# One 512-column product for the high weight instead of two of 256 columns, in five projections of a two-block transformer kernel

## The reference, cut to what matters

```python
# block 1
h = rms_norm(x, attn_norm_w[l])
proj = h @ w_cat                    # 2048 x 6448: "input projection"
y = concat([rwkv7_mixer(...), gdn_mixer(...)])
x = x + y @ w_out[l]
h = rms_norm(x, ffn_norm_w[l])
x = x + (jax.nn.silu(h @ ffn_w_gate[l]) * (h @ ffn_w_up[l])) @ ffn_w_down[l]   # gate/up: 2048 x 5632 each
# block 2
q, k, v, f_logit = split(h @ fox_w_in)        # 2048 x 6160: "fox projection"
...
up = h @ w_up                                  # 2048 x 11264
y = conv_b + conv_w[0]*pad(up)[t] + conv_w[1]*pad(up)[t+1] + conv_w[2]*pad(up)[t+2]
gate, val = split(y); out = (silu(gate) * val) @ w_down
```

## Time and profile before

| what | value |
|---|---|
| two timed runs | 2782.08 and 2787.71 us, median 2784.89 |
| the profiled execution | 2763.92 us, its span in the trace 2762.2 us, mean granted TensorE clock 0.959 of full |
| TensorE matrix products busy | 2625.6 us, 95% of the span |
| VectorE, ScalarE busy | 1494.2 us (54%), 1109.7 us (40%) |
| DMA | 421.74 MB, 153 GB/s over the span |

### The profile page before, as it was taken

One profiled execution on the slowest core, in us unless ns is written; L12 is line 12 of the kernel. 1 busy time (PEld: TensorE's weight loads), 2 busy tenths in 40 slices (PEclk: granted clock), 3 DMA queues, 4 the chain that ended last, 5 costly groups with the idle time before them and its releaser, 6 DMA issues.

```text
span 2762.2 us, 57089 instructions
## 1 busy us (share of the span) xinstructions
PE 2625.6 (95%) x24185; PEld 2545.2 (92%) x24185; DVE 1494.2 (54%) x1679; ACT 1109.7 (40%) x1050; POOL 69.2 (3%) x69
## 2 busy tenths in 40 slices
PE   7999988889899999999999799998999999999999
PEld 6999878478889999999999799986989999999999
DVE  5457567374554454444444544546456676676444
ACT  3333413231335444444333433434345555454333
POOL 1000040000100000000010000000100000000000
PEclk8999989679999999999999899997999999999999
DMA  5555200000545565555555356530545555566664
GB/s 164 188 190 186 91 2 4 1 1 27 170 153 188 194 197 189 192 197 190 193 193 178 102 196 196 188 118 1 172 160 188 196 196 187 193 197 189 193 197 153
DMA packets 169214, 421.74 MB, mean 153 GB/s; under 512 B 17462, under 2 KB 22139, under 8 KB 168859
## 3 DMA queue, kind: packets, MB, share of 16 engines
q1 hardware_dynamic: 168699, 419.13, 46.7%
q10 hardware_dynamic: 416, 1.18, 0.1%
HBM read 418.16 MB, written 2.10 MB: 152 GB/s over the span
## 4 chain that ended last, share of the span: by engine, by line
PE 88%; DVE 8%; ACT 2%; issue 1%; SPq 0%; DMA 0%; DVEq 0%; POOL 0%; ACTq 0%; POOLq 0%
PE ps L1581 25%; PE ps L1582 25%; PE ps L1583 25%; DVE LOW L879 1%; PE ps L1621 1%; PE ps L2001 1%; DVE NSQ L913 1%; ACT HIW L508 1%; PE ps L1671 1%; PE ps L1678 1%; PE ps L1705 1%; PE ps L1715 1%; PE ps L1734 1%; PE ps L1712 1%; PE ps L1969 1%
## 5 line engine op out<-in xcount | busy, mean ns | idle before, releaser
L879 DVE TENSOR_TENSOR LOW<-RAW,HIW 128x2048 fp32r<-128x2048 f32 (+2 forms) x400 | 910.4, 2276 | 1020.7 <-ACT HIW L508 1020.7
L1581 PE MATMUL ps<-H,HIW 128*128 128x256 f32 x4928 | 1373.7, 279 | 43.0 <-DVE LOW L879 21.2
L1582 PE MATMUL ps<-H,HIW 128*128 128x256 f32 x4928 | 1371.3, 278 | 0.0
L1583 PE MATMUL ps<-H,LOW 128*128 128x256 f32 x4928 | 1371.2, 278 | 0.0
L508 ACT ACTIVATE HIW<-RAW 128x2048 fp32r<-128x2048 f32 (+2 forms) x400 | 760.8, 1903 | 1202.1 <-PE ps L1583 1202.1
L1581 PEld LDWEIGHTS ps<-H,HIW 128*128 128x128 f32 x4928 | 936.0, 190 | 47.1 <-issue 26.1
L1582 PEld LDWEIGHTS ps<-H,HIW 128*128 128x128 f32 x4928 | 932.7, 189 | 0.0
L1583 PEld LDWEIGHTS ps<-H,LOW 128*128 128x128 f32 x4928 | 932.2, 189 | 0.0
L1581 PE MATMUL ps<-HID,HIW 128*128 (+1 forms) x1408 | 388.7, 276 | 1.3 <-DVE LOW L879 1.3
L1582 PE MATMUL ps<-HID,HIW 128*128 (+1 forms) x1408 | 388.6, 276 | 0.0
L1583 PE MATMUL ps<-HID,LOW 128*128 (+1 forms) x1408 | 388.6, 276 | 0.0
(11 more groups left out here) (351 smaller groups left out, 1787.7 us busy)
## 6 DMA issues: line engine op xcount, KB each, us to landing
RAW<-in_ffn_w_up SPq DMA_DIRECT2D x264, 512.0 KB, 4.5
RAW<-in_ffn_w_down SPq DMA_DIRECT2D x176, 512.0 KB, 4.6
RAW<-in_w_in SPq DMA_DIRECT2D x96, 512.0 KB, 4.2
RAW<-in_fox_w_in SPq DMA_DIRECT2D x96, 512.0 KB, 4.3
RAW<-in_ffn_w_gate SPq DMA_DIRECT2D x88, 512.0 KB, 3.8
RAW<-in_w_out SPq DMA_DIRECT2D x32, 512.0 KB, 4.9
RAW<-in_fox_w_out SPq DMA_DIRECT2D x32, 512.0 KB, 4.9
RAW<-in_w_in SPq DMA_DIRECT2D x4, 576.0 KB, 4.9
```

Source lines behind the costliest of these rows:

```text
L879: V.tensor_tensor(LOW[:, u_const % 4, 0:n], RAW[:, u_const % 4, 0:n], HIW[:, u_const % 2, 0:n].bitcast(F32), ALU.subtract).then_inc(lo_mad ...
L1581: mm(o_, hi_w, h_hi, start=start, stop=False)
L1582: mm(o_, hi_w, h_lo, start=False, stop=False)
L1583: i = mm(o_, lo_w, h_hi, start=False, stop=stop)
```

## The change

In the phases whose `group_phase` has `both=True` (IN, FOX, FFN1, FFN2), the first two products of a triple become one: the high weight tile is loaded once and meets the high and the low half of the activation tile in one product of 512 columns over the whole bank. The low weight by the high activation goes into the second half of the bank. The output tile is then the sum of the bank's two halves. For this H and HID are laid out with the two halves of a k-tile side by side. OUT, OUT2, both down projections and the small units keep three products.

The evictions change with it: ScalarE copies the second half of each bank to SBUF (`small_half`), VectorE adds the first half to it (`add_half`) and frees the bank. FFN1's silu and product, which were part of the eviction, become whole-group instructions behind units 1 and 2 (silu on ScalarE, product on VectorE), HID's parts follow behind units 3 and 4. In FFN2 tap 0 moves from VectorE to ScalarE (behind unit 1, 8 instructions with a scale and a bias per partition), the 16 instructions of the other two taps are dealt 5, 6 and 5 to units 2, 3 and 4, the silu moves to unit 5, the product to 6 and both parts of HID to 7. Two scratch tiles (ROWS, RWK) move to another place in H's memory.

```diff
-        H = at("H", [P, 2, KT, T], h0, F32R); o += 32768
+        H = at("H", [P, KT, 2, T], h0, F32R); o += 32768
...
-        HID = at("HID", [P, 2, FT, T], r2, F32R)
+        HID = at("HID", [P, FT, 2, T], r2, F32R)
...
+            def small_half(dst, f, m0, u_end, z0, g):
+                if f < GROUP - 1:
+                    act.wait_ge(tile_summed, g * 7 + (m0 + f + 1))
+                else:
+                    act.wait_ge(unit_used, g * UG + (u_end + FREE_UNITS))
+                A(dst, ps[f][:, T:2 * T], ACT.Copy).then_inc(half_out, 1)
+
+            def evac_in(g):
+                for f in range(GROUP):
+                    small_half(PR[:, bass.ds(g * 8 + (3 + f), 1), PAD:TP], f, M_IN, U_IN + UG, Z_IN, g)
...
-            group_phase(U_IN, 3)
+            group_phase(U_IN, 3, evac_in)
...
             def evac_ffn1(g):
-                for i in range(4):
-                    act.wait_ge(tile_summed, g * 7 + (M_FFN1 + 2 * i + 1))
-                    A(SG[:, i, :], ps[2 * i][:, 0:T], ACT.Silu).then_inc(S("gate_act"), 1)
+                act.wait_ge(S("hid_made"), g + 1)
+                for f in range(GROUP):
+                    small_half((SG, HS)[f % 2][:, f // 2, :], f, M_FFN1, U_FFN1 + UG, Z_FFN1, g)
 
             def tail_ffn1(g, j):
                 if j == 1:
-
-                    act.wait_ge(bank_freed, g * 8 + (N_FFN1 + 8 + FREE_BANKS))
-                    A(HID[:, 0, bass.ds(g * 4, 4), :], HS[:], ACT.Copy).then_inc(S("hid_hi"), 1)
+                    act.wait_ge(bank_freed, g * 8 + (N_FFN1 + 7 + FREE_BANKS))
+                    A(SG[:], SG[:], ACT.Silu).then_inc(S("gate_act"), 1)
+                elif j == 3:
+                    act.wait_ge(S("hid_full"), g + 1)
+                    A(HID[:, bass.ds(g * 4, 4), 0, :], HS[:], ACT.Copy).then_inc(S("hid_hi"), 1)
...
             def tail_ffn2(g, j):
-                if j == 3:
+                if j == 1:
+                    act.wait_ge(bank_freed, g * 8 + (N_FFN2 + 8 + FREE_BANKS))
+                    cb = COL["ffn_conv_b_2"]
+                    for i in range(GROUP):
+                        row = (i % 2) * FT + i // 2
+                        ins = A((YG, YV)[i % 2][:, i // 2, :], UC[:, i, 0:T], ACT.Identity,
+                                scale=vec[:, bass.ds(g * 4 + (COL["conv0"] + row), 1)],
+                                bias=vec[:, bass.ds(g * 4 + (cb + row), 1)])
+                    ins.then_inc(S("conv_step"), 1)
+                elif j == 5:
                     act.wait_ge(S("conv_step"), g * 3 + 3)
                     A(YG[:], YG[:], ACT.Silu).then_inc(S("conv_gate"), 1)
...
+            def add_half(dst, f, z0, g):
+                dve.wait_ge(half_out, g * 8 + (z0 + f + 1))
+                V.tensor_tensor(dst, dst, ps[f][:, 0:T], ALU.add).then_inc(bank_freed, 1)
+
             def evac_in(g):
                 for f in range(GROUP):
-                    summed(2, f, U_IN + UG, g)
-                    V.tensor_copy(PR[:, bass.ds(g * 8 + (3 + f), 1), PAD:TP], ps[f][:, 0:T])\
-                        .then_inc(bank_freed, 1)
+                    add_half(PR[:, bass.ds(g * 8 + (3 + f), 1), PAD:TP], f, Z_IN, g)
...
             def tail_ffn2(g, j):
-                if j in (1, 2):
-                    dve.wait_ge(S("conv_step"), g * 3 + j)
-                    for i in range(GROUP):
-                        ins = V.scalar_tensor_tensor(y(i), UC[:, i, j:j + T], tap(g, j, i), y(i), ALU.mult, ALU.add)
-                    ins.then_inc(S("conv_step"), 1)
-                elif j == 4:
+                if j in (2, 3, 4):
+                    if j == 2:
+                        dve.wait_ge(S("conv_step"), g * 3 + 1)
+                    for n in range((0, 5, 11)[j - 2], (5, 11, 16)[j - 2]):
...
-                        h_hi, h_lo = hcol(0, k), hcol(1, k)
+                        h_both = hcol(k)
+                        h_hi, h_lo = h_both[:, 0, :], h_both[:, 1, :]
                         start, stop = first and kk == 0, last and kk == len(tiles) - 1
-                        o_ = ps[f][:, 0:T]
-                        mm(o_, hi_w, h_hi, start=start, stop=False)
-                        mm(o_, hi_w, h_lo, start=False, stop=False)
-                        i = mm(o_, lo_w, h_hi, start=False, stop=stop)
+                        if both:
+                            mm(ps[f][:, :].rearrange("p (a t) -> p a t", a=2), hi_w, h_both, start=start, stop=False)
+                            i = mm(ps[f][:, T:2 * T], lo_w, h_hi, start=False, stop=stop)
+                        else:
+                            o_ = ps[f][:, 0:T]
+                            mm(o_, hi_w, h_hi, start=start, stop=False)
+                            mm(o_, hi_w, h_lo, start=False, stop=False)
+                            i = mm(o_, lo_w, h_hi, start=False, stop=stop)
```

More of the change, by code:

```diff
@@ L693, in _ @@
             got("ya_full")
-            A(H[:, 0, 0:PAIRS, :], BH[:], ACT.Copy).then_inc(S("mix_hi"), 1)
+            A(H[:, 0:PAIRS, 0, :], BH[:], ACT.Copy).then_inc(S("mix_hi"), 1)
             got("cols_made")
@@ L735, in _ @@
             got("yb_full")
-            A(H[:, 0, PAIRS:KT, :], OG[:], ACT.Copy).then_inc(S("mix_hi"), 1)
+            A(H[:, PAIRS:KT, 0, :], OG[:], ACT.Copy).then_inc(S("mix_hi"), 1)
             def ffn_phase(u0, evac, tail):
@@ L1559, in _, with h_in, hid_in, unit @@
             mm = nc.tensor.matmul
-            def h_in(part, k):
-                return H[:, part, k, :]
-            def unit(u, tiles, nf, wcol, first=False, last=False, g=None, step=0, n0=None, hcol=h_in, h_wait=None):
+            def h_in(k):
+                return H[:, k, :, :]
+            def hid_in(k):
+                return HID[:, k, :, :]
+            def unit(u, tiles, nf, wcol, first=False, last=False, g=None, step=0, n0=None, hcol=h_in, h_wait=None, both=False):
                 v = u + 1
@@ L1593, in gate_up_col, with group_phase @@
                 return kk * 1024 + (i % 2) * 512 + (i // 2) * P
-            def group_phase(u0, n0, groups, wcol=plain, k_norm=None, h_wait={}):
+            def group_phase(u0, n0, groups, wcol=plain, k_norm=None, h_wait={}, both=True):
                 with pe.Fori(0, groups) as g:
@@ L1598, in group_phase @@
                         hw = h_wait.get(j) if k_norm is None else (S("h_made"), 8 * HN[k_norm] + j + 1)
-                        unit(u0 + j, [2 * j, 2 * j + 1], GROUP, wcol, j == 0, j == UG - 1, g, UG, n0, h_wait=hw)
+                        unit(u0 + j, [2 * j, 2 * j + 1], GROUP, wcol, j == 0, j == UG - 1, g, UG, n0, h_wait=hw, both=both)
             def down(u0, n0, made0):
@@ L1606, in down @@
                         unit(b + j, [2 * j, 2 * j + 1], GROUP, plain, j == 0, n0=n0 + 8 * half,
-                             hcol=lambda part, k: HID[:, part, k, :], h_wait=(S("hid_made"), made0 + 10))
+                             hcol=hid_in, h_wait=(S("hid_made"), made0 + 10))
                     with pe.Fori(0, 4) as i:
@@ L1610, in down @@
                             unit(b + 2 + j, [4 + 2 * j, 5 + 2 * j], GROUP, plain, g=i, step=4,
[L1611 removed]
+                                 hcol=lambda k: HID[:, bass.ds(i * 8 + k, 1), :, :].rearrange("p k a t -> p (k a) t"))
                     for j in range(18, 22):
                         unit(b + j, [2 * j, 2 * j + 1], GROUP, plain, last=j == 21,
[L1614 removed]
+                             hcol=hid_in, h_wait=(S("hid_made"), made0 + 11))
             def norm(k, presummed=True):
@@ L1951, in _ @@
             got("yb_full")
-            group_phase(U_OUT, N_OUT, 2, h_wait={0: (S("mix_made"), 1), 4: (S("mix_made"), 2)})
+            group_phase(U_OUT, N_OUT, 2, h_wait={0: (S("mix_made"), 1), 4: (S("mix_made"), 2)}, both=False)
             norm(1)
@@ L2042, in _ @@
             got("att_made", 2)
-            group_phase(U_OUT2, N_OUT2, 2)
+            group_phase(U_OUT2, N_OUT2, 2, both=False)
             norm(4)
```

88 lines of the change are left out of this document (46 added, 42 removed).

## The result

| | before | after |
|---|---|---|
| timed runs | 2782.08, 2787.71 us | 2826.32, 2827.93 us |
| median | 2784.89 us | 2827.12 us |
| profiled execution, its span | 2763.92, 2762.2 us | 2826.32, 2824.6 us |

The ratio after to before is 1.0152, 95% interval 1.0106 to 1.0197: slower by 1.5% where 1.6% faster was forecast. The second is the fairer one. Over the 70 single runs of the kernel before in this document its median is 2763.5 us, and only 15 of the 70 are as slow as the two timed runs of the table.

The account below looks back on a forecast made before the run. TensorE's stream of products was taken to bound the kernel. Cheaper triples save 45.3 us, phase ends cost 2; 43.3 us off the median 2784.89 gives 2741 us, 1.6% less, range 2716 to 2772.

Parts of the forecast that it names:

- What a triple costs after: TensorE in IN, FOX, FFN1, FFN2: 512-column product 216.3 ns plus 256-column product 113.3, together 329.6 instead of 340.
- The 6.6 ns beyond the columns: Time of a 256-column product in FFN1 above its 106.7 ns of columns, read as pacing by weight loads.
- The three float32 measurements: Plain float32 products of 512, 256 and 64 columns, starting 0.43 us, 215.6 ns and 111 ns apart.
- The 111 ns of 64-column products: Distance of plain float32 products with full weight tiles, taken as the pace that weight loading sets.
- the term: Saving on TensorE in the four both=True phases: 4352 triples x 10.4 ns = 45.3 us.
- The bounds: Limits for the new triple on TensorE: 323 ns (gain 17), 333.2 (gain 6.8), or 340 (no gain).
- (e): Rival: on TensorE a 512-column float32r product runs as two of 256 with two loads, 340 ns; 2787 us; 5%.
- (a): Rival: TensorE's weight loads were hidden already, so dropping one saves only 10 to 29 us; 2758 to 2777 us; 14%.
- (b): Rival: at 34 group ends the helpers cost up to 0.5 us each, 17 us; about 2758 us; 12%.
- (d): Rival: ScalarE's copies at group ends become the bottleneck, slower; at 0.65 us per copy about 2804 us; 5%.
- The count of triples: IN, FOX, FFN1 and FFN2: 34 groups of 8 units of 16 triples, 4352 triples.
- the point named as the test: FFN1's loop in the profile after: 512-column product followed after 216 ns, the 256-column one after 113.

Follow-up runs that it names:

- The second: The changed kernel, unchanged, measured again against the kernel before: 2823.34 us against 2760.05, ratio 1.0224.
- runs 3: Products alone, no kernel, in widths of 256 to 512 columns: 113.3 ns for 256, 233.2 for 512, triple 340.0, pair 353.3.
- run 4: Products alone, no kernel, activations moved by 0 to 512 bytes: pairs 346.6 to 353.5 ns, triples 353.3 to 360.0; also 16-column weight tiles and plain float32.
- run 8: Products alone, no kernel: bf16 215.8 and 109.2 ns, float32r with 16-column weight tiles 231.7 and 117.8; triples, low weights at 64 or 192, 340.0 in 47 of 48 starts.
- run 7: Products alone, no kernel, over 8 x 8 addresses of activations and low weights: mean 349.6 ns for pairs, 354.2 for triples, none under 340.0.
- 192: The kernel before with low weights 192 bytes past a multiple of 256 instead of 64, other tiles moved along; run twice, ratios 0.9962 and 0.9951.

## Why the prediction was wrong

**The failed step** is "What a triple costs after", from "I read them as paced by weight loads" to "takes 213.3 + 3 = 216.3 ns and hides the load of the low weight; the 256-column product behind it still takes 113.3". They took 235.0 and 118.3. The 6.6 ns beyond the columns are neither the weight load's nor the instruction's: they come with the columns of float32r (runs 3, 4, 8). The three float32 measurements were read correctly and run 4 repeats those of 512 and 256 columns; but plain float32 spends two clocks per column, and says nothing of a type that streams one column per clock. The 111 ns of 64-column products lay near 113.3 by accident, as far as the runs show: loads of half the duration made 256 columns no faster. Priced as measured, the term is 4352 x (340 - 353.3) = -57.9 us against the best pace, and -47.8 against the draw of the profiled run, in place of +45.3. The base of the sum was a draw as well: 2784.89 us was the median of two slow ones, 21 us above the kernel's usual 2763.5. Against that, the kernel after (2821.6 to 2827.9 us) is some 60 us slower. In the two profiled runs 47.8 us of it are the pairs and 17.5 us the untouched triples.

**The bounds were too narrow on one side.** The last of them, "no better than two, 340, no gain", excluded a loss without a row that did. The row existed: windows in IN at 117.2 ns would have shown that 340 was not the price of a triple but one of two, and would have set the lower end at 353, a loss.

**The rivals.** (e) had the sign of the wide product nearly right (no gain) but 340 for 353. (a) would have given 333 to 338 for the pair. The Trainium skill's rule (TensorE: Matmul & The Clock Gate, section Back-to-back issue gap: N/2.4 + 2.5 ns) would have given 325.0. By that rule bf16 products take 215.8 and 109.2, and run 8 measured exactly this; for float32r the runs have 226.7 to 235 and 113.3 to 118.3, and disagree. (b) and (d) didn't happen: no waits in the loops.

**What held.** The count of triples; that TensorE's stream sets the time; the evictions' distances within 0.1 us per instruction; nothing at the group ends in the loops (in FFN2 with the luck told above); and the point named as the test, the distance behind a 512-column product, which showed the error at a glance.

**What stays open.** Why float32r at one column per clock falls short by a sixteenth or more, and why by the address. Bf16 has half the bytes per column and float32 or the 1.2 GHz level half the columns per ns, and all three lose nothing that grows with the columns, which would suit a supply of 4-byte columns that can't quite keep up at 2.4 GHz; that is argued, not shown. Nor is it known what decides the draw after a pause, why 192 draws well in the kernel when it didn't differ from 64 in run 8, why triples at 0 and 64 took 340 in runs 3, 7 and 8 and 353.3 in run 4, and whether pairs would pay in a kernel at an address where triples don't reach 340.

## What to carry to other kernels

Before costing fewer, wider matrix products, measure the pair's distance at the kernel's own type and addresses: for float32r at 2.4 GHz, time goes by columns and addresses. Dropping instructions and weight loads bought nothing here against triples at their best address; against triples at most other addresses of run 7 it saved a few ns in 350. Read the distance between products in every phase of the trace, not in one; two paces in one trace mean that the price being improved on is a draw. When a kernel's runs spread by 1 to 2%, try its operands' offsets modulo 256 bytes before its schedule.

## What the runs showed of the hardware

- At 2.4 GHz a float32r stream settles after a pause, here within about a dozen products, and keeps its pace until the next: 113.3 or 117.8 ns per 256 columns at the kernel's addresses, others elsewhere. A hitch of 0.16 us changed it once. None was under 17 clocks for 16 columns.
- The 512-column product costs more per column at most addresses (233.3) and as much as two of 256 at best (226.7); 320, 384 and 448 columns lie between 17.3 and 17.7 clocks for 16.
- At the 1.2 GHz level nothing is lost. Start of FOX in the kernel after, by timeline and by stretch (granted clock 0.50):

```profile
1592.44 0.41 PE L1616 MATMUL ps<-H,LOW 128*128 128x256 f32 x1
1592.65 0.63 PE L1615 MATMUL ps<-H,HIW 128*128 128x512 f32 x1
1593.08 0.41 PE L1616 MATMUL ps<-H,LOW 128*128 128x256 f32 x1
```

```profile
1592.00:1594.00 2.00, 2.00 (x8) 1.71 (x8) 1.35 (x1) 0.00 (x0) 0.00 (x0) 0.50 1.01 391
```

0.21 us for 256 columns and 0.43 for 512 are the columns at 1.2 GHz and no more (213.3, 426.7).
